# Two transformer blocks on one core: a raw turn ahead of the second MLP, an earlier first split, small loads on another queue, and a norm turned in smaller helpings

## The reference

```python
h_lat = modulate(rms_norm_2(x, norm_mix_g[l]), sh_m, sc_m)
h_ctx = modulate(rms_norm_2(y, norm_mix_g[l]), csh_m, csc_m)
p_lat = h_lat @ w_in[l]
p_ctx = h_ctx @ w_in[l]
...
x = x + gt_m * (jnp.concatenate([hg_lat, at_lat], axis=-1) @ w_out[l])
x = x + gt_f * swiglu(modulate(rms_norm_2(x, norm_ffn_g[l]), sh_f, sc_f),
                      w_gate_up[l], w_down[l])
```

## Time and profile before

| | us |
|---|---|
| median of 3 runs | 2791.94 |
| lowest, highest | 2787.03, 2792.59 |
| the profiled execution | 2788.66 |
| its span in the profile | 2786.8 |
| TensorE busy in it | 2711.8 (97%), 13606 matmuls |
| VectorE busy | 1838.4 (66%) |
| ScalarE busy | 1260.3 (45%) |
| GpSimd busy | 59.0 (2%) |
| read from HBM | 568.16 MB, 205 GB/s over the span |

### The profile page before, as it was taken

The page is one execution under the profiler, slowest core; times in us unless marked ns, Lnnn a source line. Parts: engine busy times, 40 slices in busy tenths (PEclk is TensorE's granted clock), DMA queues, the critical chain, the costliest instruction groups (busy, mean ns, idle before and its releaser), DMA issues.

```text
span 2786.8 us, 34261 instructions
## 1 busy us (share of the span) xinstructions
PE 2711.8 (97%) x13606; PEld 2285.6 (82%) x13606; DVE 1838.4 (66%) x2461; ACT 1260.3 (45%) x1646; POOL 59.0 (2%) x80
## 2 busy tenths in 40 slices
PE   7999999999999999999999999999989999999999
PEld 6899889878888888888788788877768888888887
DVE  5657766576888888766766765666666666554555
ACT  3333555554434434455555455444344444434433
POOL 0000000000000000000000000101000000000000
PEclk9999999999999999999999999999999999999999
DMA  6766655467777777856676645343347777566565
GB/s 215 251 229 227 197 174 174 157 222 259 245 264 257 248 262 245 298 188 212 196 236 221 227 144 159 121 130 120 100 135 248 255 245 241 179 193 192 187 194 174
DMA packets 303311, 572.51 MB, mean 205 GB/s; under 512 B 20428, under 2 KB 30048, under 8 KB 303024
## 3 DMA queue, kind: packets, MB, share of 16 engines
q1 hardware_dynamic: 299712, 559.77, 61.9%
q0 software_dynamic: 3264, 10.49, 1.3%
q10 hardware_dynamic: 176, 0.07, 0.0%
HBM read 568.16 MB, written 2.10 MB: 205 GB/s over the span
## 4 chain that ended last, share of the span: by engine, by line
PE 87%; DVE 5%; ACT 3%; DMA 3%; issue 2%; SPq 0%; DVEq 0%; ACTq 0%
PE ps L1637 24%; PE ps L1639 24%; PE ps L1638 23%; PE ps L1631 2%; PE ps L1633 2%; PE ps L1632 2%; DMA raw<-in_w_in 2%; PE ps L1592 2%; ACT whi L1904 2%; DVE wlo L2186 1%; PE ps L1840 1%; PE ps L1820 1%; PE ps L1649 1%; PE ps L1702 1%; DVE acc L2204 1%
## 5 line engine op out<-in xcount | busy, mean ns | idle before, releaser
L2186 DVE TENSOR_TENSOR wlo<-raw,whi 128x1024 fp32r<-128x1024 f32 x857 | 1044.1, 1225 | 693.6 <-ACT whi L1904 684.9
L1904 ACT ACTIVATE whi<-raw 128x1024 fp32r<-128x1024 f32 x857 | 899.8, 1056 | 1039.5 <-PE ps L1639 300.0
L1637 PE MATMUL ps<-whi,th 128*128 128x512 f32 (+2 forms) x3168 | 1255.9, 396 | 34.5 <-DVE wlo L2186 19.9
L1639 PE MATMUL ps<-whi,tl 128*128 128x512 f32 (+2 forms) x3168 | 1231.9, 389 | 0.0
L1638 PE MATMUL ps<-wlo,th 128*128 128x512 f32 (+2 forms) x3168 | 1230.7, 388 | 0.0
L1637 PEld LDWEIGHTS ps<-whi,th 128*128 128x128 f32 x3168 | 601.7, 190 | 159.0 <-DVE wlo L2186 25.0
L1639 PEld LDWEIGHTS ps<-whi,tl 128*128 128x128 f32 x3168 | 601.5, 190 | 124.5
L1638 PEld LDWEIGHTS ps<-wlo,th 128*128 128x128 f32 x3168 | 602.5, 190 | 117.7 <-issue 1.9
L2204 DVE SCALAR_TENSOR_TENSOR acc<-raw,silc,acc 128x512 f32<-128x512 f32 x480 | 344.4, 748 | 58.8 <-DMA raw<-in_w_mod 53.9
L1631 PE MATMUL ps<-th,whi 128*128 128x256 f32 x640 | 188.2, 294 | 4.1 <-DVE wlo L2186 4.1
L1632 PE MATMUL ps<-th,wlo 128*128 128x256 f32 x640 | 183.6, 287 | 0.0
(11 more groups left out here) (276 smaller groups left out, 1407.9 us busy)
## 6 DMA issues: line engine op xcount, KB each, us to landing
raw<-in_w_in SPq DMA_DIRECT2D x240, 512.0 KB, 3.8
raw<-in_w_down SPq DMA_DIRECT2D x216, 512.0 KB, 4.4
raw<-in_w_mod SPq DMA_DIRECT2D x192, 512.0 KB, 3.8
raw<-in_w_gate_up SPq DMA_DIRECT2D x176, 512.0 KB, 3.5
raw<-in_w_up SPq DMA_DIRECT2D x128, 512.0 KB, 4.0
raw<-in_w_out SPq DMA_DIRECT2D x64, 512.0 KB, 3.8
raw<-in_xattn_wkv SPq DMA_DIRECT2D x16, 512.0 KB, 3.8
raw<-in_xattn_wq SPq DMA_DIRECT2D x8, 512.0 KB, 3.7
```

The source lines that it names most:

```text
L1637: pe.matmul(p, xh, wh[:, c, c0:n], start=a and (form == "rows" or tb == 0), stop=False, skip_group_check=True)
L1639: ins = pe.matmul(p, xl, wh[:, c, c0:n], start=False, stop=z, skip_group_check=True)
L1904: self.e.activation(t.his[g % NHI][:, 0:n], t.raws[j % NRAW][:, 0:n], ACT.Copy).then_inc(*s.hi.up(g))
L2186: self.e.tensor_tensor(t.los[j % NRAW][:, 0:n], t.raws[j % NRAW][:, 0:n], t.his[g % NHI][:, 0:n].bitcast(F), ALU.subtract).then_inc(*s.lo. ...
```

## The change

1. **Start.** `op1.gen` is stepped twice, one chunk is split by `prepare()`, then it is stepped twice more. A new attribute `lead` holds the split back: at chunk n at most `min(3, n + lead)` chunks are ahead. `first_steps` begins after piece 5: a square in each of two steps, the root in the next, and three steps later `columns_rest` together with the spread; `late_loads` follows one step after.
2. **Queues.** The nine late loads, and `ones` and `mskt`, go from SP's queue to GpSimd's, behind a wait for the low part of piece 5 of x.
3. **Last norm.** Its turn gets `rest=1`, so a quarter comes in every fourth step, not every second.
4. **Second MLP's input.** `raw_turn` turns x of "lat1" without its token factors, while the output product still runs: quarter q two steps after its residual, times the columns' gain, to a new tile `yr` (16 x 256, float32, in the place of `tl1`). When all is added, the factors are made and spread over a bank, copied to `rsb_ffn`; the last quarter is turned; and `settle` finishes two kt at a time: VectorE multiplies by the factors, ScalarE adds the shift and rounds to the high part, VectorE adds the shift and subtracts the high part. A chunk needs its own two kt only (`grain`). `mod_gain` moves ahead of the last parts.

```diff
+        self.grain = lambda kt: 2 * (kt // 4 + 1)
...
+        self.yr = sb("yr", r_1 + 16384, [16, S])
...
-        self.load_consts()
...
-                if self.g > self.gn + LOOK:
+                if self.g > self.gn + min(LOOK, self.gn + self.lead):
...
-        while op.pieces < 2 * (kt // 4 + 1):
+        while op.pieces < op.grain(kt):
...
+    def raw_turn(self, name, op, g, gtok, order, st):
+
+        s = self.s
+        for q in order:
+            while (st, q) not in self.flags:
+                yield
+            while not op.hurry and self.ticks < self.rn_at[q] + 2:
+                yield
+            for tb in range(2):
+                while not (self.big.ready() or self.side_ready()):
+                    yield
+                j, bank = 2 * q + tb, (self.big if self.big.ready() else self.side()).take()
+                self.raw_piece(name, j, bank, op, g, gtok)
+                self.xb[j] = self.xb[j] + [(s.tp, (name, j))]
+                bank.give((s.tg, (name, j)))
+            yield
+
+    def settle(self, name, op, sh, shtok):
+
+        s = self.s
+        op.grain, op.pieces = lambda kt: kt // 2 + 1, 0
+        self.settle_scale(name, 0, op)
+        for p in range(8):
+            if p < 7:
+                self.settle_scale(name, p + 1, op)
+            for kt in (2 * p, 2 * p + 1):
+                self.settle_halves(name, kt, op, sh, shtok)
+                op.ready[kt] = [(s.tl, (name, kt))]
+            op.pieces = p + 1
+            yield
+
...
-                  t.mod[:, 0:16], [(s.gs, "lat")] + self.mod_cols(0, 4), ease=True)
+                  t.mod[:, 0:16], [(s.gs, "lat")] + self.mod_cols(0, 4), rest=1, ease=True)
...
-        for _ in range(3):
+        for _ in range(2):
             next(op1.gen)
+        self.prepare()
+        for _ in range(2):
+            next(op1.gen)
+        self.lead = 1
         self.spawn("small", op1.gen)
 
         def first_steps():
+            landed = [w for v in self.xb for w in v if w[0] in s.ld_x]
+            while op1.pieces < 5:
+                yield
+            for tb in range(2):
+                self.stat("x", tb, t.x, landed, 2)
+                self.xn_after = [[(s.sq, ("x", tb))] for _ in range(4)]
+                yield
+            op1.rs = self.rstd("x", 2)
+            for _ in range(3):
+                yield
             slot = self.side().take()
             self.columns_rest(slot.tile)
             slot.give((s.cols, "cols"), (s.cols, "cols2"), (s.cols, "bmc"))
             self.stgs.after = [[(s.ini, "rest")], [(s.ini, "rest")]]
-            yield
+            self.spread("x", op1.rs)
             yield
             self.late_loads()
-            yield
-            op1.rs = self.stats("x", t.x, [w for v in self.xb for w in v], 2)
-            self.spread("x", op1.rs)
             for _ in range(6):
                 yield
...
+        self.mod_gain("ffn", t.gmod[:, 0, :], t.mod[:, 64:80], t.gain["ffn2"], self.mod_cols(16, 20), [(s.tg, ("ctx", 7))])
+        opf = Operand(t.op["1"], op1.end)
         for n in (2, 3):
             pairs[n] = self.take_pair()
...
+        raw = self.raw_turn("ffn", opf, t.gmod[:, 0, :], [(s.gs, "ffn")], (2, 3, 0, 1), "lat1")
+        self.spawn("small", raw)
...
         rs = self.sums("ffn", 14)
-        opf = Operand(t.op["1"], op1.end)
-        at = [list(v) for v in self.xb]
-        self.turn("ffn", self.x_part, lambda q, tb: at[2 * q + tb], rs, opf, t.gmod[:, 0, :], t.mod[:, 48:64], [(s.gs, "ffn")] + self.mod_cols(12, 16), whole=False)
-        for _ in range(3):
+        self.spread("ffn", rs)
+        opf.hurry = True
+        for _ in raw:
+            pass
+        self.drain("small")
+        opf.hurry = False
+        opf.gen = self.settle("ffn", opf, t.mod[:, 48:64], self.mod_cols(12, 16))
+        for _ in range(2):
             next(opf.gen)
...
+    def late_loads(self):
+        t, s, a, cd, po = self.t, self.s, self.a, self.a["consts"], self.e
+        self.wait_ge(*s.tl.at(("x", 5)))
+        po.dma_start(t.lmk[:, :], cd[:, LMK:LMK + 256]).then_inc(*s.ld_late.up("lmk", 16))
...
+    def settle_halves(self, name, kt, op, sh, shtok):
+        s = self.s
+        self.wait_ge(*s.ts.at((name, kt // 2)))
+        self.wait_all(shtok)
+        self.e.activation(op.h[:, kt, :], self.t.yr[:, kt, :], ACT.Identity, bias=sh[:, kt:kt + 1]).then_inc(*s.th.up((name, kt)))
...
+    def settle_scale(self, name, p, op):
+        s, y = self.s, self.t.yr[:, 2 * p:2 * p + 2, :]
+        self.wait_ge(*s.sd.at(name))
+        for tb in range(2):
+            self.wait_ge(*s.tg.at((name, 2 * (p // 2) + tb)))
+        self.e.tensor_tensor(y, y, self.t.rsb[name][:, :].unsqueeze(1).broadcast_to([128, 2, S]), ALU.mult).then_inc(*s.ts.up((name, p)))
+
+    def settle_halves(self, name, kt, op, sh, shtok):
+        s = self.s
+        self.wait_ge(*s.th.at((name, kt)))
+        self.e.scalar_tensor_tensor(out=op.l[:, kt, :], in0=self.t.yr[:, kt, :], scalar=sh[:, kt:kt + 1],
+                                    in1=op.h[:, kt, :].bitcast(F), op0=ALU.add, op1=ALU.subtract).then_inc(*s.tl.up((name, kt)))
```

More of the change, by code:

```diff
@@ L249, in __init__ @@
         self.xq = sb("xq", z + 32768, [4, S])
-        self.rsb = {"x": sb("rsb_x", r_m + 5120, [S]), "xa": sb("rsb_xa", r_y, [S]), "mem": sb("rsb_mem", r_y + 1024, [S])}
+        self.rsb = {"x": sb("rsb_x", r_m + 5120, [S]), "xa": sb("rsb_xa", r_y, [S]), "mem": sb("rsb_mem", r_y + 1024, [S]),
+                    "ffn": sb("rsb_ffn", r_y, [S])}
         self.xn = sb("xn", r_s, [D])
@@ L341, in skip @@
         pass
-    start_loads = load_mem_part = load_consts = columns_rest = spread_rstd = mem_square = heads_direct = finish = load_x_part = late_loads = load_ctx = load_final = load_masks = load_bounds = load_qkg = skip
-    issue = columns = split = mod_add = mod_total = multiply = turn_scale = turn_piece = turn_low = stat = root = reduce_sums = skip
+    start_loads = load_mem_part = columns_rest = spread_rstd = mem_square = heads_direct = finish = load_x_part = late_loads = load_ctx = load_final = load_masks = load_bounds = load_qkg = skip
+    issue = columns = split = mod_add = mod_total = multiply = turn_scale = turn_piece = raw_piece = settle_scale = settle_halves = turn_low = stat = root = reduce_sums = skip
     heads_silu = rows_out = residual_add = spatial_weights = skip
@@ L564, in stats, with rstd @@
             self.xn_after = [[(self.s.sq, (name, tb))] for _ in range(4)]
+        return self.rstd(name, at)
+    def rstd(self, name, at):
         self.root(name, self.t.st[:, at:at + 2], D, [(self.s.sq, (name, 0)), (self.s.sq, (name, 1))])
         return [(self.t.st[:, at + tb:at + tb + 1], (self.s.rs, name)) for tb in range(2)]
-    def after_pieces(self, op, gen):
-        while op.pieces < 8:
-            yield
-        yield from gen
     def sums(self, name, at):
@@ L703, in epi @@
                     self.rn_at[n] = self.ticks
+                    self.flags.add((st, n))
             pair.give(*freed)
@@ L1167, in first_steps @@
             slot.give((s.wt, 0))
-        self.spawn("load", self.after_pieces(op1, first_steps()))
+        self.spawn("load", first_steps())
         w_in = a["w_in"][0]
@@ L1654, in turn_piece, with raw_piece @@
         self.wait_all(here)
+        self.wait_all(bank.after)
+        self.turn4(bank.tile, [xp[:, 128 * i:128 * i + 128] for i in range(4)]).then_inc(*self.s.tp.up((name, j)))
+    def raw_piece(self, name, j, bank, op, g, gtok):
+        q, tb = j // 2, j % 2
+        xp = self.x_part(q, tb)
+        self.wait_ge(*self.s.res.at(("lat1", q, tb)))
         self.wait_all(bank.after)
@@ L1880, in spread_rstd @@
         self.wait_ge(*s.sp.at(name))
-        if name != "x":
+        if name == "ffn":
+            self.wait_ge(*s.q7.at("lq1"))
+        elif name != "x":
             self.wait_ge(*s.gv5.at(1))
@@ L2245, in turn_low, with raw_piece @@
         self.e.tensor_tensor(op.l[:, at[0], at[1]], y, op.h[:, at[0], at[1]].bitcast(F), ALU.subtract).then_inc(*s.tl.up((name, j)))
+    def raw_piece(self, name, j, bank, op, g, gtok):
+        s, q, tb = self.s, j // 2, j % 2
+        self.wait_ge(*s.tp.at((name, j)))
+        self.wait_all(gtok)
+        self.wait_all(op.used)
+        self.e.tensor_tensor(self.t.yr[:, 4 * q:4 * q + 4, 128 * tb:128 * tb + 128], bank.tile[:, :].rearrange("p (a b) -> p a b", a=4),
+                             bc(g[:, 4 * q:4 * q + 4], 128), ALU.mult).then_inc(*s.tg.up((name, j)))
+    def settle_scale(self, name, p, op):
[9 more added lines that the diff above has]
+                                    in1=op.h[:, kt, :].bitcast(F), op0=ALU.add, op1=ALU.subtract).then_inc(*s.tl.up((name, kt)))
     def residual_add(self, key, pair, end, slot, last, out):
```

29 lines of the change are left out of this document (11 added, 18 removed).

## The result

The changed kernel takes 2773.62 us (median of 4 runs, 2770.43 to 2779.19) against 2790.11 for the kernel before (4 runs): ratio 0.9944, 95% interval 0.9924 to 0.9964. The forecast was 2774.7. The profiled execution took 2773.37, its span 2771.6, against 2788.66 and 2786.8: 15.3 us less, where 17.2 were forecast. The forecast of 2774.7 started from the median of three runs before, 2791.9; with the fourth it is 2790.1, so by the medians 16.5 us were won. TensorE's granted clock is 0.987 on average in both.

What follows compares the result with a forecast made beforehand. TensorE was taken to bound the kernel (87% of the work that ends last), gaining only where it stalls or runs at half clock. -6.0 - 2.5 - 8.7 = -17.2 us gave 2771.5 profiled, 2774.7 as median; range 2762 to 2785.

Steps and rivals of the forecast that it cites:

- Start: First two products: +1.6 us at the first product's end, -9.75 for a stall removed, +2.1 for a new wait; sum -6.0.
- Last norm: Turning of the last norm beside the context products: -8.2 us of losses gained, +5.7 for a new wait; sum -2.5.
- Seam: Second output product to gate/up product: 40.1 us before, 31.4 after, first matmul 7.8 us after the last; sum -8.7 us.
- its half clock: Behind each TensorE wait over 2 us, here chunk 6's: 1.6 us lost to matmuls running at half clock.
- The gain of 9.75: Behind the first product: TensorE's 7.41 us wait for wlo goes, and the next chunk takes 2.76 instead of 5.1 us.
- the new wait of 2.1 us ahead of the compression: After the first product: cmp_blocks ends 11 us behind it, TensorE's spread and three chunks 8.9, so TensorE waits 2.1 us.
- The rival of transfers (B): Start bound by transfers: it brings -2 us instead of -6.0, total 2778.7; chance 0.17.
- The backlog's term: Last norm, 1320.2 to 1376.2 us: waits and half clock beyond 47.8 us of work vanish, gaining 8.2 us.
- The hand-over: End of last norm's turn: next product waits for a PSUM pair's hV copies, 4.1 us plus 1.6 of half clock.
- Rival C: Last norm: PSUM pair's hand-over is hidden or short, so the whole 8.2 us is gained, total 2769.0; chance 0.13.
- D: Last norm's backlog stays and the pair's hand-over costs as forecast; start -2, seam -5: total 2786.6; chance 0.09.
- Rival E: First three products: TensorE stays at 1.2 GHz, 2.3 us per chunk; ten chunks give 2797.7, twelve 2802.3; chance 0.04.

Runs made afterwards that it cites:

- e4: The changed kernel with its eleven late loads issued by SP again, at the same place and without their wait for tl: 2782.57 us, ratio 0.9971 to the kernel before.
- e7: The changed kernel with the last norm's quarters at steps 0, 4, 8 and 10 instead of 0, 4, 8 and 12: 2774.34 us, ratio 0.9940 to the kernel before.
- e10: The changed kernel with the last norm's quarters at steps 0, 3, 6 and 8 instead of 0, 4, 8 and 12: 2772.15 us, ratio 0.9930.
- e12: The changed kernel with the last norm's quarters at steps 0, 3, 6, 8, and squares and root one place earlier on ScalarE: 2767.39 us, ratio 0.9904.

## Why the prediction was right, and where not

**The total** was right by 1.1 us, in part by luck: errors cancel, and the kernel before was 1.8 us faster by its new median than the forecast took it to be. Start: -6.0 forecast; measured as the lead at 69 us, 8.2 in the changed kernel and 8.7 on average over the five kernels with its start (7.4 to 11.0), against 0 and 1.5 for the two with the start of before: -8. Last norm: -2.5 forecast, +0.4 measured. Seam: -8.7 forecast, -8.1 measured. Sum of these -15.7, against 15.6 by the ratio of the medians. The parts are less certain than their sum: at 323 us the same five kernels lead by 7.4 on average and those two by 0 and 1.0, so the start is then worth 7. One sum of the prediction is off too: its bounds of the parts, two at an end at once, give 2763 to 2783, not 2762 to 2787; the measured time lies within either.

**Start.** First matmul 11.0 forecast, 11.21; chunk 6 waits 2.5 forecast, 2.45; its half clock 1.6 forecast, and the chunk takes 4.6 instead of 2.9 (35.23 to 39.84), 1.7; end of the product 42.6 forecast, 42.9. The gain of 9.75 behind it came in full: from the start of the second product to the mark at 69 us it was 28.0 us before and is 17.6 now, 10.4 less. The step that failed is the new wait of 2.1 us ahead of the compression: there is none. I let TensorE wait for the end of all of cmp_blocks, 11 us behind the product. But `cmp_hidden` waits for `s.cb.at((m, 1, 1))` with m = 0 first, the fourth of its eight operations:

```profile
48.80 3.94 DVE L2435 TENSOR_TENSOR cb<-cc,cols 128x240 f32<-128x240 f32 x8
```

The fourth ends at 50.8 in the changed kernel, and the compression starts at 51.44 without waiting, while the eighth runs till 52.74. In e4 the fourth ends at 57.0 and TensorE starts at 57.06. So the path exists and is 0.6 us from being the limit here. The four later operations, 1.9 us, are nearly all of the 2.1 that I charged; besides, cmp_blocks ends 9.8 us behind the product and not 11. Without that term the sum is -8.1. The rival of transfers (B) fell for the changed kernel: whi waited 1.81 us for its chunk and TensorE not at all, though e4 shows how near it was. (The Trainium skill, ScalarE: Activation LUTs, What ACT_TABLE_LOAD costs, would have had chunk 7 wait 1.4 us. The root's ACTIVATE again starts 1.30 us behind the load, 34.37 to 35.67: the trace does not agree with it here. That no wait stands between 35.23 and 43.15 would not show it alone, since chunk 6 at half clock ends late enough to cover 1.4 us.)

**Last norm.** The backlog's term was right (8.4 of 8.2). The hand-over was under-sized: 4.1 us of waiting forecast, 6.25 measured; the half clock behind it cost 1.6 as forecast (12 matmuls in 4.36 us, from 1363.49 to 1367.85, instead of 2.72). I had put the first yb right behind its bar, at 1356.7. But on VectorE the accumulations of a modulation chunk stood in front, behind 0.66 us of waiting for that chunk, and yb starts at 1358.98, 2.3 us later. So 7.9 stand against 8.4, and at 1415 comes a wait of 1.19 us for wlo that the kernel before doesn't have: next to nothing is left. Rival C, a hidden hand-over, fell, and so did D, a backlog that stays; e7 and e10 show that hiding the hand-over uncovers the gate.

**Seam.** First matmul 7.8 forecast, 7.7; the half clock cost 2.4 instead of 1.6 (twelve matmuls from 2027.44 to 2032.56, 5.1 us, all of the chunk and not seven tenths). From 2019.7 to the end of the seventh chunk, 2048.9, are 29.2 us; with the 2.7 of the six bars that is 31.9, where 31.4 were forecast and 40.1 stood before. At hV and chunk 6 the charge was right. ScalarE has no xn there and TensorE no wait for tl behind the first chunk: forecast and seen.

**Clock.** Rival E, 1.2 GHz for ten more chunks, fell: from 40 to 60 us the granted clock of the changed kernel is 1.00 throughout, where the one before had 0.52 from 50 to 60; only from 35 to 40, behind the wait of 2.45 us, is it 0.66. The stretch at 0.50 that spoke for E is there in every kernel, before and after (below), and TensorE waits for nothing from 141 to 195 us in any of them.

## What to carry to other kernels

Find the stall first by asking which instruction stands ahead of the one that TensorE waits for, on each queue: here a factor behind a transfer behind nine small loads. With either of the two edits taken back the lead at 69 us was -1.3 and 0.6 us, with both in place 8. Put work without a deadline ahead of an instruction that waits anyway, not behind it: two squares of 2 us each stood behind th in the changed kernel and ahead of it in e12, and there the second product began 4.6 us sooner. Before crediting the end of a backlog, look what the work that is now later was holding, here a PSUM pair, and add the rest of the same step on the engine that must free it.

## What had not been expected of the hardware

The largest difference found between two executions of the same code is TensorE's clock. The changed kernel and e7 are the same up to 1300 us, and TensorE waits 7.9 us in each between 69 and 325 us, and yet e7 loses 4.1 us of lead from 69 to 323 us and the changed kernel wins 1.1. TensorE's busy time between these two marks, for as many matmuls, holds all of the 5.2 us: 244.85 us in the changed kernel and 250.04 in e7. The first line of each fence is that stretch, the others are windows in it (busy time of PE, PEld, DVE, ACT and POOL, then PEclk, DMA share, GB/s), of the changed kernel, then of e7:

```profile
60.75:314.23 253.48, 244.85 (x1757) 232.04 (x1757) 171.51 (x303) 101.79 (x167) 2.16 (x3) 0.95 0.71 228
120.00:130.00 10.00, 10.00 (x86) 10.00 (x85) 6.73 (x9) 3.15 (x4) 0.00 (x0) 1.00 0.54 179
170.00:180.00 10.00, 10.00 (x48) 10.00 (x48) 0.00 (x0) 0.45 (x2) 0.00 (x0) 0.50 0.11 28
230.00:240.00 10.00, 8.59 (x62) 8.58 (x62) 7.45 (x16) 3.59 (x4) 0.00 (x0) 0.83 0.59 183
```

```profile
60.69:319.35 258.66, 250.04 (x1757) 235.74 (x1757) 171.86 (x303) 101.85 (x167) 2.16 (x3) 0.93 0.70 224
120.00:130.00 10.00, 9.75 (x70) 9.75 (x71) 6.81 (x10) 4.25 (x5) 0.00 (x0) 0.83 0.47 149
170.00:180.00 10.00, 10.00 (x48) 10.00 (x48) 1.39 (x2) 1.49 (x3) 0.00 (x0) 0.50 0.00 0
230.00:240.00 10.00, 8.38 (x47) 8.18 (x47) 7.58 (x15) 4.22 (x5) 0.00 (x0) 0.68 0.61 206
```

At 170 to 180 us both run at 0.50, which is 1.2 GHz, with PE busy for all 10 us (every kernel here has 0.50 to 0.55 in one window of 10 us between 170 and 190); at 120 and 230 e7 has 0.83 and 0.68 where the other has 1.00 and 0.83. Ten us at 0.68 instead of 0.83 are 1.5 us, at 0.83 instead of 1.00 1.7: 3.2 of the 5.2 that part the two. What decides it no run here shows, nor whether a kernel with a faster start gives some of it back there as a rule. It makes a single trace uncertain by some 5 us in this stretch, as much as a part of this change.
